# Gate products of the recurrent branch: stacked hi and lo fp32r products of a 64-channel block in place of fp32 products with block diagonal weights

## The chip, the cores and the metric

The kernel runs on one core of one Trainium2 chip. The metric is the device time of one execution in microseconds. A time named here is either the median of three runs or that of one profiled execution, and the text says which.

## What is computed

The reference is one layer of a hybrid decoder for 1040 prompt tokens (16 meta tokens ahead of 1024) and, separately, for eight running sequences of one token each. The kernel handles them side by side as 1050 columns (two are padding). The part that matters here is the recurrent branch (RG-LRU): a short causal convolution gives `xc`; two gates r and i come from `xc` by small dense products inside blocks of 64 channels; then a linear recurrence runs along the tokens.

```python
def _rglru(x, h0, wa, ba, wx, bx, lam):
    xb = xf.reshape(B, T, RG_BLOCKS, RG_BW)          # 16 blocks of 64 channels
    r = sigmoid(einsum('btnc,ncd->btnd', xb, wa) + ba)
    i = sigmoid(einsum('btnc,ncd->btnd', xb, wx) + bx)
    log_a = -RG_C * r * softplus(-lam)
    a = exp(log_a)
    b = sqrt(-expm1(2.0 * log_a)) * (i * xf)
    b = b.at[:, 0].add(a[:, 0] * h0)
    _, h = associative_scan(_lin_comb, (a, b), axis=1)
```

Around it stand a gated linear attention branch (GLA) on 128-token chunks, the merge of both branches, and a gated feed-forward block. All weights and activations are fp32.

## The kernel before, in words

The layout has channels on the 128 partitions and tokens along the free axis, so 1024 channels are eight blocks of 128. The large weight matrices come in 149 units of 128 output channels by 1024 input channels. For each unit a weight tile is fetched (`w_raw`), ACT copies it to an fp32r tile `w_hi` (`w_high`, line 795), and DVE subtracts to get the rest, `w_lo` (`w_low`, line 1196). PE (`tile_products`, line 417) then adds up three fp32r products, hi by hi, hi by lo and lo by hi, for three column groups of 346 or 350 columns each. A unit's result lies in `acc0` or `acc1`, three PSUM banks each, which alternate from unit to unit; before a unit may start, its `acc` must have been read out (semaphore `acc_free`).

The change lies in a loop of eight turns, one for each block j of 128 channels of the recurrent branch. Each turn also does one 128-token chunk of GLA and one running sequence, cut into small pieces that PE does between the eight tiles of a unit. The order of each engine is written out by hand: PE's turn is in the loop over `NPAIR` behind `gate_product` (line 604), ACT's and DVE's are two functions that are both called `rg_body`. In one turn of before:

- PE does unit `U_RG` (the x of the recurrent branch, into acc1) and unit `U_RG+1` (its gelu partner, into acc0). Behind tiles 3 and 4 of the latter stand `O_pair` (GLA's outputs of heads 0 and 1, and of heads 2 and 3, into the banks `small6` and `small7`), behind tiles 6 and 7 the state products `dS_piece`. Then follow the r gate as three fp32 products into acc1 (line 608), a small column sum (`onorm_piece`, line 547), and the i gate as three fp32 products into acc0. The next turn's first unit goes into acc1 again.
- DVE evacuates the x unit into `rg_ext`, masks GLA's scores (line 1317), does three convolution steps (line 1443) on the tile that ACT started (line 995), subtracts the next weights (line 1196), copies both O results to SBUF (`o_copy`, line 1323), updates GLA's state (line 1330), sums the squares (line 1337), evacuates the gelu partner into `rg_gelu_ha` (line 1224), and finishes the state and another weight subtraction. At the start of a turn it scales the O of the chunk before (line 1344) and carries out the recurrence of the block before (`rg_tail_w`, `rg_tail_b`, `rg_tail_h`; the last product is line 1413).
- ACT does the exponentials of GLA and of the block before, starts the convolution (line 995), copies weights (line 795), squares O (line 895), and ends the turn with the gelu (line 1005), a weight copy, the tanh of r out of acc1 (line 1009, which frees acc1), a tanh on r (line 1013), the tanh of i out of acc0 (line 1017), a table load, and GLA's reciprocal root (lines 901 and 905).

The gate weights `gw` of a block are 128 by 256: for each of the two gates a 128 by 128 matrix with two 64 by 64 blocks on its diagonal and zeros elsewhere.

```python
unit(U_RG + 1, ..., 0, G_RG[0] + 2 * j, XH, XL, {
    ...
    3: [lambda: O_pair(0, sb6)], 4: [lambda: O_pair(1, sb7)],
    6: [lambda: dS_piece(sb6, n, PAIR, 0)], 7: [lambda: dS_piece(sb7, n, PAIR, 1)]})
pe.wait_ge(xc_step, 4 * j + 4)
gate_product(1, G_RG[1] + 2 * j + 1, 0)
onorm_piece(n, PAIR)
gate_product(0, G_RG[0] + 2 * j + 1, 1)
```

Of the kernel before, what the change touches and what calls it, by code (L numbers as in the profile page):

```python
# [93 lines left out]
def view3(t):  # L94

    return t.rearrange("p (a n) -> p a n", a=3)
# [16 lines left out]
def build(nc, I, O):  # L113
    ctx = ExitStack()
    with ctx:  # L115
# [31 lines left out]
        xc = nxt("rg_xc_h", C)  # L147
        rt = nxt("rg_r", C)
        it = nxt("rg_i_b", C)
        av = nxt("rg_a", C)  # L150
# [18 lines left out]
        gw = nxt("rg_gate_weights", 2 * P)  # L169
        sS = nxt("smp_state", H * DV)  # L170
        svb = nxt("smp_v_rows", D)
        svt = svb
# [6 lines left out]
        h0 = nxt("rg_h0", KB * NS)  # L179
        der = nxt("rg_derived", 5 * KB)  # L180
        gbz = nxt("gla_bias", H)
        sqk = nxt("smp_qk", 8 * NS)
        sdec = nxt("smp_decay", H * NS)
        srv = nxt("smp_rinv", H * NS)
# [17 lines left out]
        T = [at(f"tmp{i}", T0 + TB * i, C) for i in range(3)]  # L202
        sqsum = T[2]
        sq1 = (rt, it, av, th)

        act_bytes = (2 * GRP * CB + 31) // 32 * 32
        AH = at("act_hi", A0, 2 * GRP * C, F32R)
# [34 lines left out]
        def sem(n):  # L242
            return ctx.enter_context(nc.semaphore(n))
# [20 lines left out]
        def squares(w):  # L264
# [39 lines left out]
        xbias_ready, xc_step, rgo_kept, gelu_ready, th_ready, a_ready, a2_ready, w_ready, ml_done, m_ready = (  # L304
            sem(n) for n in ("xbias_ready", "xc_step", "rgo_kept", "gelu_ready", "th_ready", "a_ready",
                             "a2_ready", "w_ready", "ml_done", "m_ready"))
        ix_ready, b_ready, h_step, ha_ready, ha_stored = (
            sem(n) for n in ("ix_ready", "b_ready", "h_step", "ha_ready", "ha_stored"))

# [101 lines left out]
        def _(pe):  # L411
# [189 lines left out]
                                              sqk[:, bass.ds(h * NS + j, 1)], start=True, stop=True)  # L601
                mm.then_inc(so_mm, 1)

            def gate_product(g, n_grp, half):

                pe.wait_ge(acc_free[g], n_grp)
                for n in range(3):
                    mm = nc.tensor.matmul(accv[g][:, n], gw[:, half * P:(half + 1) * P], xc[:, n * NW:(n + 1) * NW],
                                          start=True, stop=True)
                mm.then_inc(gate_mm, 1)  # L610

            with pe.Fori(0, NPAIR) as j:
                n = j + 1
                zn = j + 2

                def zg_pair():
                    pe.wait_ge(ones_done, 1)
                    pe.wait_ge(olog_done, n)
                    for h in range(H):  # L620
                        mm = nc.tensor.matmul(sb6[:, h * PAIR:(h + 1) * PAIR], wg[0:R2, h * DK:(h + 1) * DK],
                                              glr[0:R2, bass.ds(NMETA + PAIR * j, PAIR)], start=True, stop=True)
                    mm.then_inc(zg_mm, 1)

# [12 lines left out]
                unit(U_RG + 1, nth(U_RG + 1, 2, j), 0, G_RG[0] + 2 * j, XH, XL, {  # L637
                    1: [lambda: keT_piece(n, PAIR, so_ready, j + 1), lambda: A_piece(n, PAIR, z_ready, zn + 1)],
                    3: [lambda: O_pair(0, sb6)], 4: [lambda: O_pair(1, sb7)],
                    6: [lambda: dS_piece(sb6, n, PAIR, 0)], 7: [lambda: dS_piece(sb7, n, PAIR, 1)]})  # L640
                pe.wait_ge(xc_step, 4 * j + 4)
                pe.wait_ge(gwt_loaded, 16 * j + 16)
                gate_product(1, G_RG[1] + 2 * j + 1, 0)
                pe.wait_ge(S_ready, 2 * n + 1)
                onorm_piece(n, PAIR)
                gate_product(0, G_RG[0] + 2 * j + 1, 1)

            def onorm_samples():

# [129 lines left out]
        def _(act):  # L779
# [4 lines left out]
            def plain():  # L784

                act.wait_ge(ones_done, 1)
# [190 lines left out]
            def rg_body(j, first, last):  # L978
# [11 lines left out]
                if not last:  # L990
# [4 lines left out]
                nc.scalar.activation(xc, ext[:, 3:3 + C], ACT.Identity, scale=par("w3", j), bias=par("b", j))\  # L995
                    .then_inc(xbias_ready, 1)
                w_high(U_RG + 2, 2, j)
                act.wait_ge(sS_ready, j + 1)
                act.dma_start(O["gla_sample"][j], sS).then_inc(sS_stored, 16)
                if not last:  # L1000
                    rg_prefetch(j)
                o_square(n, PAIR, NMETA + PAIR * j, 0)
                o_square(n, PAIR, NMETA + PAIR * j, 1)
                act.wait_ge(acc_free[0], G_RG[0] + 2 * j + 1)
# [1 line left out]
                w_high(U_RG + 3, 2, j)  # L1006
                plain()
                act.wait_ge(gate_mm, 2 * j + 1)
                nc.scalar.activation(view3(rt), accv[1], ACT.Tanh, scale=0.5, bias=col(der, j)).then_inc(acc_free[1], 1)
                plain()  # L1010
                act.wait_ge(acc_free[1], G_RG[1] + 2 * j + 2)
                act.wait_ge(b_ready, j)
                nc.scalar.activation(th, rt, ACT.Tanh, scale=col(der, j + 4 * KB), bias=col(der, j + 4 * KB)).then_inc(th_ready, 1)
                plain()
                act.wait_ge(gate_mm, 2 * j + 2)
                act.wait_ge(h_step, 4 * j)
                nc.scalar.activation(view3(it), accv[0], ACT.Tanh, scale=0.5, bias=col(der, j + KB)).then_inc(acc_free[0], 1)
# [162 lines left out]
        def _(dve):  # L1180
# [234 lines left out]
            def rg_body(j, first):  # L1415
# [13 lines left out]
                nc.vector.tensor_copy(V3[:, :, bass.ds(NT + j, 1)], hd(sb7, 8, 1)).then_inc(so_ready, 1)  # L1429
                if not first:  # L1430
                    rg_tail_h(j - 1)
                    dve.wait_ge(xc_step, 4 * j)
# [3 lines left out]
                scores(n, PAIR)  # L1436
                c0 = NMETA + PAIR * j

                dve.wait_ge(xbias_ready, j + 1)
                dve.wait_ge(acc_free[1], G_RG[1] + 2 * j + 1)  # L1440
# [340 lines left out]
```

## Time and profile before

| | us |
|---|---|
| median of three runs | 1923.3 |
| the three runs | 1923.18, 1924.96, 1923.30 |
| the profiled execution, its own time | 1920.77 |
| its span, first to last instruction | 1919.0 |
| PE busy in it (matmuls) | 1890.9 |
| DVE busy | 921.1 |
| ACT busy | 565.7 |

The profile is of one execution. Busy times are shares of the whole span, over stages that differ; a matmul's displayed duration holds its way through the array, so that successive ones overlap, and the pace of PE is read from the distance of their starts. An fp32 matmul shows as two records of the same line. The timeline lists instructions by start and duration, and names in brackets what an engine waited for.

### The profile page before, as it was taken

Reading aid. Unit: us, or ns where it says so; the run is one execution under the profiler, and the core shown is the slowest. Engines: PE = TensorE matmul, PEld = TensorE weight load, DVE = VectorE, ACT = ScalarE, POOL = GpSimd, SP = SyncE. Lnnn points to the kernel's source line nnn. Section 1 sums busy time; section 2 is a strip of 40 time slices with the busy share of each in tenths; the row PEclk is TensorE's granted clock in tenths of the full one; section 3 lists DMA queues with packets and bytes.
Section 4 is the critical chain, followed back from the end, with each engine's and each line's share of the span. In section 5 each row is a group of like instructions: output and inputs, shape, how many; then the busy total and the mean of one; then the engine's idle time right before and its main releaser. Section 6 shows DMA issues by size and latency. Waiting matters only on the chain. (4 is left out here: it accounts for less than half of the span.)

```text
span 1919.0 us, 28820 instructions
## 1 busy us (share of the span) xinstructions
PE 1890.9 (99%) x11866; PEld 1860.3 (97%) x11866; DVE 921.1 (48%) x1067; ACT 565.7 (29%) x630; POOL 27.6 (1%) x24
## 2 busy tenths in 40 slices
PE   7999999999999999999999999999999999999998
PEld 6999899999999999999999999999999999999997
DVE  6221377788754222422244455545453545455455
ACT  5010256755642111211132332222121212131225
POOL 0000000000000000000000000000000000000032
PEclk9999999999999999999999999999999999999999
DMA  5221132223111111311131111111111111111112
GB/s 196 97 76 52 37 110 104 93 79 134 63 61 44 55 44 44 133 44 47 51 133 44 56 45 46 53 45 45 45 45 44 55 45 45 44 44 50 44 58 89
DMA packets 48234, 126.72 MB, mean 66 GB/s; under 512 B 7000, under 2 KB 20184, under 8 KB 48144
## 3 DMA queue, kind: packets, MB, share of 16 engines
q1 hardware_dynamic: 27808, 87.97, 13.6%
q10 hardware_dynamic: 20352, 37.64, 5.6%
q8 instruction: 62, 1.02, 0.2%
q14 instruction: 12, 0.10, 0.0%
HBM read 107.71 MB, written 18.14 MB: 66 GB/s over the span
## 5 line engine op out<-in xcount | busy, mean ns | idle before, releaser
L417 PE MATMUL acc<-xn_hi,w_hi 128*128 128x346 f32 (+1 forms) x2496 | 814.6, 326 | 2.5 <-issue 2.2
L417 PE MATMUL acc<-xn_lo,w_hi 128*128 128x346 f32 (+1 forms) x2496 | 803.6, 322 | 0.0
L417 PE MATMUL acc<-xn_hi,w_lo 128*128 128x346 f32 (+1 forms) x2496 | 801.5, 321 | 0.0
L417 PEld LDWEIGHTS acc<-xn_hi,w_hi 128*128 128x128 f32 x2496 | 470.9, 189 | 6.2 <-issue 3.4
L417 PEld LDWEIGHTS acc<-xn_lo,w_hi 128*128 128x128 f32 x2496 | 472.4, 189 | 1.5
L417 PEld LDWEIGHTS acc<-xn_hi,w_lo 128*128 128x128 f32 x2496 | 471.0, 189 | 0.0
L795 ACT ACTIVATE w_hi<-w_raw 128x1024 fp32r<-128x1024 f32 x149 | 156.4, 1050 | 460.2 <-PE acc L417 459.1
L1196 DVE TENSOR_TENSOR w_lo<-w_raw,w_hi 128x1024 fp32r<-128x1024 f32 x149 | 182.4, 1224 | 182.0 <-ACT w_hi L795 181.9
L417 PE MATMUL acc<-act_hi,w_hi 128*128 128x344 f32 x504 | 161.7, 321 | 2.6 <-DVE residual L1610 2.6
L417 PE MATMUL acc<-act_hi,w_lo 128*128 128x344 f32 x504 | 161.6, 321 | 0.0
L417 PE MATMUL acc<-act_lo,w_hi 128*128 128x344 f32 x504 | 161.6, 321 | 0.0
L1610 DVE TENSOR_TENSOR residual<-acc,residual 128x1032 f32<-128x1032 f32 x56 | 68.9, 1231 | 99.2 <-PE acc L417 99.2
L417 PEld LDWEIGHTS acc<-act_hi,w_hi 128*128 128x128 f32 x504 | 95.3, 189 | 4.6 <-DVE residual L1610 4.6
L417 PEld LDWEIGHTS acc<-act_lo,w_hi 128*128 128x128 f32 x504 | 95.1, 189 | 0.0
L417 PEld LDWEIGHTS acc<-act_hi,w_lo 128*128 128x128 f32 x504 | 94.8, 188 | 0.0
L1224 DVE TENSOR_TENSOR tmp<-acc,rms 128x1038 f32<-128x1038 f32 x24 | 29.7, 1239 | 134.8 <-PE acc L417 134.7
L1576 DVE TENSOR_TENSOR val_ext<-acc,rms 128x1038 f32<-128x1038 f32 x24 | 29.7, 1239 | 82.3 <-PE acc L417 82.3
L1115 ACT ACTIVATE gate_conv<-gate_ext,ffn_params 128x1032 f32<-128x1032 f32 x24 | 30.0, 1250 | 127.7 <-DVE gate_ext L1576 127.7
L1128 ACT ACTIVATE act_hi<-tmp 128x1032 fp32r<-128x1032 f32 x24 | 25.6, 1069 | 135.0 <-DVE tmp L1595 135.0
L1576 DVE TENSOR_TENSOR gate_ext<-acc,rms 128x1038 f32<-128x1038 f32 x24 | 29.7, 1239 | 72.2 <-PE acc L417 63.2
L1581 DVE SCALAR_TENSOR_TENSOR gate_conv<-gate_ext,ffn_params,gate_conv 128x1024 f32<-128x1024 f32 x48 | 61.5, 1282 | 2.9 <-DVE gate_conv L1581 0.9
L1581 DVE SCALAR_TENSOR_TENSOR tmp<-val_ext,ffn_params,tmp 128x1024 f32<-128x1024 f32 x48 | 61.5, 1282 | 2.8 <-DVE tmp L1581 0.2
(229 smaller groups left out, 2209.2 us busy)
## 6 DMA issues: line engine op xcount, KB each, us to landing
w_raw<-in_w SPq DMA_DIRECT2D x152, 512.0 KB, 3.5
ha_scratch<-rg_gelu_ha ACTq DMA_DIRECT2D x8, 519.0 KB, 2.7
h<-ha_scratch ACTq DMA_DIRECT2D x8, 519.0 KB, 6.1
residual<-in_x ACTq DMA_DIRECT2D x8, 519.0 KB, 6.4
gla_qk_pair<-qk_scratch ACTq DMA_DIRECT2D x8, 512.0 KB, 4.5
smp_v_rows<-smp_v_scratch ACTq DMA_DIRECT2D x8, 512.0 KB, 5.7
out_gla_sample<-smp_state ACTq DMA_DIRECT2D x8, 512.0 KB, 3.1
smp_state<-in_gla_state ACTq DMA_DIRECT2D x7, 512.0 KB, 4.9
```

What stands on the lines that cost most here:

```text
L417: mm = nc.tensor.matmul(acc[g][:, n, 0:cw], w[s][:, t * P:(t + 1) * P], x[:, c0 + n * cw:c0 + (n + 1) * cw], start=a, stop=z)
L795: nc.scalar.activation(whi[s], raw[s], ACT.Copy).then_inc(w_hi_done[s], 1)
L1115: nc.scalar.activation(cg[:, down_c], eg[:, 2 + D0:2 + D1], ACT.Identity, scale=fpr[:, bass.ds(2 * UB + F, 1)], bias=fpr[:, bass.ds(3 * UB ...
L1128: nc.scalar.activation(blkd(AH, half * GRP + f), act_t[:, down_c], ACT.Copy).then_inc(acth_done, 1)
L1196: nc.vector.tensor_tensor(wlo[s], raw[s], whi[s].bitcast(F32), ALU.subtract).then_inc(w_split[s], 1)
L1224: nc.vector.tensor_tensor(view3(out), acc[g][0:n_part, :, 0:cw], view3(rms[0:n_part, c0:c0 + 3 * cw]), ALU.mult)\
L1576: nc.vector.tensor_tensor(view3(e_t[:, 2 + L0:2 + L1]), accl[g], view3(rms[:, late]), ALU.mult).then_inc(acc_free[g], 1)
L1581: nc.vector.scalar_tensor_tensor(c_t[:, D0:NT], e_t[:, D0 + t:t + NT], fpr[:, bass.ds(t * UB + off_b + F, 1)], c_t[:, D0:NT], ALU.mult, AL ...
L1610: nc.vector.tensor_tensor(view3(blkd(X2, m)), accd[g], view3(blkd(X2, m)), ALU.add).then_inc(acc_free[g], 1)
```

## The change

The gate weights now come from the host in another arrangement: for each 64-channel block the weights of both gates stand side by side (64 input channels by 128 outputs), once on partitions 0 to 63 and once more on 64 to 127. For the second block the order of the two gates is turned round, and the bias of the i gate is stored with its halves swapped. ACT makes the fp32r tile `gwh` of them and DVE the rest `gwl`. From `xc` ACT makes the high part of the first block (partitions 0 to 63, tile `xsa`) and of the second (64 to 127, tile `xsb`), and DVE puts the low part of each on the other 64 partitions of the same tile. The two tiles lie over `rg_a` and `rg_mult`.

A gate product then gives both gates of one block: per column group one product of `gwh` over 128 partitions (hi weights by hi and lo activations at once) and one of `gwl` over the 64 partitions with the hi activations. The result has 64 partitions of r and 64 of i, so ACT reads it with four tanh on 64 partitions in place of two on 128.

`o_copy` moves from DVE to ACT, `O_pair` moves one tile later on PE, and DVE masks the scores ahead of the evacuation of the x unit instead of behind it.

```diff
+        xsa, xsb = at("xc_hi_lo", rt_at + 2 * xc_size, C, F32R), at("xc_lo_hi", rt_at + 3 * xc_size, C, F32R)
...
-            def gate_product(g, n_grp, half):
+            def gate_product(g, n_grp, xs, half, c0):
 
                 pe.wait_ge(acc_free[g], n_grp)
                 for n in range(3):
-                    mm = nc.tensor.matmul(accv[g][:, n], gw[:, half * P:(half + 1) * P], xc[:, n * NW:(n + 1) * NW],
-                                          start=True, stop=True)
+                    c = slice(n * NW, (n + 1) * NW)
+                    nc.tensor.matmul(accv[g][:, n], gwh[:, c0:c0 + P], xs[:, c], start=True, stop=False)
+                    mm = nc.tensor.matmul(accv[g][:, n], gwl[half, c0:c0 + P], xs[half, c], start=False, stop=True)
                 mm.then_inc(gate_mm, 1)
...
-                    3: [lambda: O_pair(0, sb6)], 4: [lambda: O_pair(1, sb7)],
+                    4: [lambda: O_pair(0, sb6)], 5: [lambda: O_pair(1, sb7)],
...
-                pe.wait_ge(xc_step, 4 * j + 4)
-                pe.wait_ge(gwt_loaded, 16 * j + 16)
-                gate_product(1, G_RG[1] + 2 * j + 1, 0)
+                pe.wait_ge(gw_split, j + 1)
+                pe.wait_ge(xs_split, 2 * j + 1)
+                gate_product(1, G_RG[1] + 2 * j + 1, xsa, slice(0, HP), 0)
                 pe.wait_ge(S_ready, 2 * n + 1)
                 onorm_piece(n, PAIR)
-                gate_product(0, G_RG[0] + 2 * j + 1, 1)
+                pe.wait_ge(xs_split, 2 * j + 2)
+                gate_product(0, G_RG[0] + 2 * j + 1, xsb, slice(HP, P), P)
...
                 w_high(U_RG + 2, 2, j)
+                act.wait_ge(gwt_loaded, 16 * j + 16)
+                nc.scalar.activation(gwh, gw, ACT.Copy).then_inc(gw_hi_done, 1)
...
+                o_copy(n, PAIR, NMETA + PAIR * j, 0, sb6)
+                o_copy(n, PAIR, NMETA + PAIR * j, 1, sb7)
+                act.wait_ge(xc_step, 4 * j + 4)
+                nc.scalar.activation(xsa[0:HP], xc[0:HP], ACT.Copy).then_inc(xs_hi_done, 1)
+                nc.scalar.activation(xsb[HP:P], xc[HP:P], ACT.Copy).then_inc(xs_hi_done, 1)
                 o_square(n, PAIR, NMETA + PAIR * j, 0)
                 o_square(n, PAIR, NMETA + PAIR * j, 1)
...
                 act.wait_ge(gate_mm, 2 * j + 1)
-                nc.scalar.activation(view3(rt), accv[1], ACT.Tanh, scale=0.5, bias=col(der, j)).then_inc(acc_free[1], 1)
+                act.wait_ge(h_step, 4 * j)
+                nc.scalar.activation(view3(rt[0:HP]), accv[1][0:HP], ACT.Tanh, scale=0.5, bias=der[0:HP, bass.ds(j, 1)])
+                nc.scalar.activation(view3(it[0:HP]), accv[1][HP:P], ACT.Tanh, scale=0.5, bias=der[HP:P, bass.ds(j + KB, 1)])\
+                    .then_inc(acc_free[1], 1)
...
-                o_copy(n, PAIR, c0, 0, sb6)
-                o_copy(n, PAIR, c0, 1, sb7)
+                dve.wait_ge(gw_hi_done, j + 1)
+                nc.vector.tensor_tensor(gwl, gw, gwh.bitcast(F32), ALU.subtract).then_inc(gw_split, 1)
+                dve.wait_ge(xs_hi_done, 2 * j + 1)
+                nc.vector.tensor_tensor(xsa[HP:P], xc[0:HP], xsa[0:HP].bitcast(F32), ALU.subtract).then_inc(xs_split, 1)
+                dve.wait_ge(xs_hi_done, 2 * j + 2)
+                nc.vector.tensor_tensor(xsb[0:HP], xc[HP:P], xsb[HP:P].bitcast(F32), ALU.subtract).then_inc(xs_split, 1)
                 state(n, PAIR, 0, sb6)
...
```

The order of ACT at the end of a turn, from the gelu's table load to the next one, before (`w_hi_55` is the second weight slot, `acc` either accumulator):

```order
L1005 ACT_TABLE_LOAD
L1005 ACTIVATE rg_gelu_ha<-rg_gelu_ha 128x1038
L795 ACTIVATE w_hi_55<-w_raw_53 128x1024
L1009 ACTIVATE rg_r<-acc,rg_derived 128x1050
L1013 ACTIVATE rg_mult<-rg_r,rg_derived 128x1050
L1017 ACTIVATE rg_i_b<-acc,rg_derived 128x1050
L1018 ACT_TABLE_LOAD
```

The same place now:

```order
L1026 ACT_TABLE_LOAD
L1026 ACTIVATE rg_gelu_ha<-rg_gelu_ha 128x1038
L804 ACTIVATE w_hi_55<-w_raw_53 128x1024
L1031 ACTIVATE rg_r<-acc,rg_derived 64x1050
L1032 ACTIVATE rg_i_b<-acc,rg_derived 64x1050
L1036 ACTIVATE rg_r<-acc,rg_derived 64x1050
L1038 ACTIVATE rg_i_b<-acc,rg_derived 64x1050
L1043 ACTIVATE rg_mult<-rg_r,rg_derived 128x1050
L1044 ACT_TABLE_LOAD
```

Two tanh of 128 partitions have become four of 64, and the tanh on r (`rg_mult<-rg_r`), which stood between the two, now stands behind all four.

The order of DVE from the end of the convolution to the evacuation of the gelu partner, before:

```order
L1447 COPY rg_last_columns<-rg_ext 128x13
L1196 TENSOR_TENSOR w_lo_58<-w_raw_54,w_hi_56 128x1024
L1323 COPY v_o<-small 128x4x128 x2
L1330 SCALAR_TENSOR_TENSOR gla_state<-gla_state,gla_exp_bc,small 128x256 x2
L1337 TENSOR_TENSOR gla_z_g_osq<-gla_z_g_osq 128x4x128
L1224 TENSOR_TENSOR rg_gelu_ha<-acc,rms 128x1038
```

And now:

```order
L1473 COPY rg_last_columns<-rg_ext 128x13
L1222 TENSOR_TENSOR w_lo_58<-w_raw_54,w_hi_56 128x1024
L1476 TENSOR_TENSOR rg_gate_weights_lo<-rg_gate_weights,rg_gate_weights_hi 128x256
L1478 TENSOR_TENSOR xc_hi_lo<-rg_xc_h,xc_hi_lo 64x1050
L1480 TENSOR_TENSOR xc_lo_hi<-rg_xc_h,xc_lo_hi 64x1050
L1356 SCALAR_TENSOR_TENSOR gla_state<-gla_state,gla_exp_bc,small 128x256 x2
L1363 TENSOR_TENSOR gla_z_g_osq<-gla_z_g_osq 128x4x128
L1250 TENSOR_TENSOR rg_gelu_ha<-acc,rms 128x1038
```

The two copies of O are gone from DVE, and three subtractions, one of gate weights and two of 64 partitions of activations, stand ahead of the state update and of that evacuation.

## Rows read from the trace of the kernel before

**Rows 1.** The page's part 1, PE: busy us (share of span) and instructions.

```profile
PE 1890.9 (99%) x11866; PEld 1860.3 (97%) x11866; DVE 921.1 (48%) x1067; ACT 565.7 (29%) x630; POOL 27.6 (1%) x24
```

**Rows 2.** Timeline of PE, end of one turn: start us, us, engine, line, operation.

```profile
480.10 0.32 PE L417 MATMUL acc<-xn_lo,w_hi 128*128 128x346 f32 x1
480.26 0.32 PE L417 MATMUL acc<-xn_hi,w_lo 128*128 128x346 f32 x1
...
483.57 1.93 PE L608 MATMUL acc<-rg_xc_h,rg_gate_weights 128*128 128x350 f32 x6
485.34 1.02 PE L547 MATMUL small<-gla_z_g_osq,ones 128*128 128x512 f32 x2
486.19 1.93 PE L608 MATMUL acc<-rg_xc_h,rg_gate_weights 128*128 128x350 f32 x6
487.69 0.59 PE L417 MATMUL acc<-xn_hi,w_hi 128*128 128x350 f32 x1
```

**Rows 3.** Timeline of ACT, the same turn.

```profile
472.32 1.26 ACT L995 ACTIVATE rg_xc_h<-rg_ext,params 128x1050 f32<-128x1050 f32 x1
...
484.25 1.07 ACT L1005 ACTIVATE rg_gelu_ha<-rg_gelu_ha 128x1038 f32<-128x1038 f32 x1 [1.51 <-DVE rg_gelu_ha L1224]
485.22 1.04 ACT L795 ACTIVATE w_hi<-w_raw 128x1024 fp32r<-128x1024 f32 x1
486.17 1.12 ACT L1009 ACTIVATE rg_r<-acc,rg_derived 128x1050 f32<-128x1050 f32 x1
487.47 1.27 ACT L1013 ACTIVATE rg_mult<-rg_r,rg_derived 128x1050 f32<-128x1050 f32 x1 [0.18 <-issue]
488.64 1.12 ACT L1017 ACTIVATE rg_i_b<-acc,rg_derived 128x1050 f32<-128x1050 f32 x1
489.78 1.28 ACT L1018 ACT_TABLE_LOAD   x1
```

**Rows 4.** Timeline of DVE, the same turn and the next one's O scaling.

```profile
455.06 1.23 DVE L1344 TENSOR_TENSOR v_o<-v_o,gla_qd 128x1024 f32 x1 [2.65 <-ACT gla_qd L905]
...
469.06 1.23 DVE L1413 TENSOR_TENSOR rg_gelu_ha<-rg_xc_h,rg_gelu_ha 128x1038 f32<-128x1038 f32 x1
...
471.37 0.75 DVE L1317 COPY_PREDICATED gla_scores<-causal_mask,small 128x512 f32<-128x512 int32 x1
...
478.20 1.22 DVE L1196 TENSOR_TENSOR w_lo<-w_raw,w_hi 128x1024 fp32r<-128x1024 f32 x1
479.34 1.28 DVE L1323 COPY v_o<-small 128x512 f32 x2
481.48 0.87 DVE L1330 SCALAR_TENSOR_TENSOR gla_state<-gla_state,gla_exp_bc,small 128x256 f32<-128x256 f32 x2 [0.86 <-PE small L540]
...
482.98 1.24 DVE L1224 TENSOR_TENSOR rg_gelu_ha<-acc,rms 128x1038 f32<-128x1038 f32 x1
...
493.05 1.23 DVE L1344 TENSOR_TENSOR v_o<-v_o,gla_qd 128x1024 f32 x1 [2.64 <-ACT gla_qd L905]
```

**Rows 5.** Lines L830 and L1230 (min/median/max ns), groups by line (busy us, mean ns).

```profile
L830 ACT ACTIVATE gla_low_rank<-acc x1: 1039/1039/1039, 24.1 to 24.1; 32x1050 f32<-32x1050 f32 x1
L1230 DVE TENSOR_TENSOR gla_low_rank<-gla_low_rank,rms x1: 1241/1241/1241, 39.3 to 39.3; 32x1050 f32<-32x1050 f32 x1
L875 ACT ACTIVATE gla_v_tokens<-small 128x512 f32<-128x512 f32 x16 | 9.4, 587 | 3.0 <-PE small L503 3.0
L1379 DVE TENSOR_SCALAR smp_state<-smp_state,smp_decay 128x256 f32<-128x256 f32 x32 | 9.1, 348 | 0.0
```

**Rows 6.** Stretches of 2 us: busy us by engine, granted TensorE clock, DMA share, GB/s.

```profile
210.00:212.00 2.00, 0.29 (x3) 0.28 (x4) 1.98 (x2) 1.32 (x2) 0.00 (x0) 1.00 0.00 0
...
218.00:220.00 2.00, 0.99 (x5) 0.98 (x5) 0.82 (x2) 0.26 (x1) 0.00 (x0) 0.62 0.00 0
...
222.00:224.00 2.00, 2.00 (x10) 1.94 (x9) 0.00 (x0) 0.60 (x1) 0.00 (x0) 0.50 0.00 0
224.00:226.00 2.00, 2.00 (x10) 2.00 (x10) 0.00 (x0) 0.00 (x0) 0.00 (x0) 0.67 0.70 231
```

More of the change, by code:

```diff
@@ L32 @@
 NMETA = 16
+HP = P // 2
 SEQ = 1024
@@ L147, in build @@
         xc = nxt("rg_xc_h", C)
+        rt_at, xc_size = off[0], (CB + 31) // 32 * 32
         rt = nxt("rg_r", C)
@@ L168, in build @@
         glr = nxt("gla_low_rank", C)
-        gw = nxt("rg_gate_weights", 2 * P)
+        gw_at = off[0]
+        gw, gwl = nxt("rg_gate_weights", 2 * P), at("rg_gate_weights_lo", gw_at, 2 * P, F32R)
         sS = nxt("smp_state", H * DV)
@@ L181, in build @@
         gbz = nxt("gla_bias", H)
+        gwh = nxt("rg_gate_weights_hi", 2 * P, F32R)
         sqk = nxt("smp_qk", 8 * NS)
@@ L306, in build @@
                              "a2_ready", "w_ready", "ml_done", "m_ready"))
+        gw_hi_done, gw_split, xs_hi_done, xs_split = (sem(n) for n in ("gw_hi_done", "gw_split", "xs_hi_done", "xs_split"))
+        r_ready = sem("r_ready")
         ix_ready, b_ready, h_step, ha_ready, ha_stored = (
@@ L890, in ke_tokens, with o_copy @@
                 nc.scalar.activation(bc[0:w, :], sb7[0:w, :], ACT.Copy).then_inc(keT_ready, 1)
+            def o_copy(n, w, c0, hh, bank):
+                plain()
+                act.wait_ge(O_mm, 2 * n + hh + 1)
+                nc.scalar.activation(V3[:, 4 * hh:4 * hh + 4, bass.ds(c0, w)], hd(bank, 4, w), ACT.Copy).then_inc(o_copied, 1)
             def o_square(n, w, c0, hh):
@@ L1008, in rg_body @@
                 act.wait_ge(gate_mm, 2 * j + 1)
-                nc.scalar.activation(view3(rt), accv[1], ACT.Tanh, scale=0.5, bias=col(der, j)).then_inc(acc_free[1], 1)
+                act.wait_ge(h_step, 4 * j)
+                nc.scalar.activation(view3(rt[0:HP]), accv[1][0:HP], ACT.Tanh, scale=0.5, bias=der[0:HP, bass.ds(j, 1)])
+                nc.scalar.activation(view3(it[0:HP]), accv[1][HP:P], ACT.Tanh, scale=0.5, bias=der[HP:P, bass.ds(j + KB, 1)])\
+                    .then_inc(acc_free[1], 1)
                 plain()
+                act.wait_ge(gate_mm, 2 * j + 2)
+                nc.scalar.activation(view3(rt[HP:P]), accv[0][HP:P], ACT.Tanh, scale=0.5, bias=der[HP:P, bass.ds(j, 1)])\
+                    .then_inc(r_ready, 1)
+                nc.scalar.activation(view3(it[HP:P]), accv[0][0:HP], ACT.Tanh, scale=0.5, bias=der[0:HP, bass.ds(j + KB, 1)])\
+                    .then_inc(acc_free[0], 1)
+                act.wait_ge(r_ready, j + 1)
                 act.wait_ge(acc_free[1], G_RG[1] + 2 * j + 2)
@@ L1013, in rg_body @@
                 nc.scalar.activation(th, rt, ACT.Tanh, scale=col(der, j + 4 * KB), bias=col(der, j + 4 * KB)).then_inc(th_ready, 1)
[L1014 to L1017, printed above, removed]
                 act.preload_act_table_set(LN_EXP)
@@ L1431, in rg_body @@
                     rg_tail_h(j - 1)
+                scores(n, PAIR)
+                if not first:
                     dve.wait_ge(xc_step, 4 * j)
@@ L1435, in rg_body @@
                 evacuate(U_RG, 2, j, 1, ext[:, 3:3 + C])
-                scores(n, PAIR)
-                c0 = NMETA + PAIR * j
                 dve.wait_ge(xbias_ready, j + 1)
@@ L1725 @@
     x = np.ascontiguousarray(tokens.T.reshape(KB, P, C))
-    vecs = [a["rg_conv_w"][0][i] for i in range(4)] + [a["rg_conv_b"][0], a["rg_ba"][0], a["rg_bx"][0],
+    vecs = [a["rg_conv_w"][0][i] for i in range(4)] + [a["rg_conv_b"][0], a["rg_ba"][0], a["rg_bx"][0].reshape(KB, 2, HP)[:, ::-1].reshape(-1),
             a["rg_lambda"][0], a["norm1_g"][0], a["gla_norm_g"][0].reshape(-1), a["norm2_g"][0], a["final_norm_g"]]
-    gates = np.zeros((KB, P, 2, P), f32)
-    for c, w in enumerate((a["rg_wa"][0], a["rg_wx"][0])):
-        w = w.reshape(KB, 2, 64, 64)
-        gates[:, 0:64, c, 0:64] = w[:, 0]
-        gates[:, 64:128, c, 64:128] = w[:, 1]
+    wa, wx = (a[n][0].reshape(KB, 2, HP, HP) for n in ("rg_wa", "rg_wx"))
+    pairs = np.stack([np.concatenate([wa[:, 0], wx[:, 0]], axis=2), np.concatenate([wx[:, 1], wa[:, 1]], axis=2)], axis=2)
+    gates = np.ascontiguousarray(np.concatenate([pairs, pairs], axis=1))
     t = np.arange(P)
```

## The prediction

> **What bounds the kernel now.** I read the page's busy times first: PE is busy 99% of the span [rows 1], so at first sight whatever shortens PE's stream shortens the run. That share is an average, so I then read one turn of the loop over the eight 128-channel blocks, where the change lies, on three timelines: PE, ACT, DVE. A turn takes 37.99 us: DVE scales the same O tile at 455.06 and again at 493.05 [rows 4]. PE has no idle mark in it. At the end of a turn come the two fp32 gate products [rows 2], then the next unit's first product, displayed at 487.69 but advancing only when the second gate product ends, about 487.95 (486.19 plus 1.77).
>
> The reader should now see how thin the cover is. That next unit accumulates into the same three banks (acc1) as the first gate product, so it waits until ACT has read the product out. ACT reads it at 486.17 for 1.12 us, done at 487.29 [rows 3]: 0.66 us before PE needs it. ACT is not late because the product is (it ended near 485.4) but because gelu and a weight copy stand ahead of the tanh in its queue: gelu starts at 484.25, when DVE's evacuation of 482.98 (1.24 us) ends [rows 3, 4]. Here, not in PE's busy share, a change of this loop is decided.
>
> **PE's products.** Each fp32 gate product (three column groups) takes 485.34 - 483.57 = 1.77 us of PE [rows 2]. It becomes six products at fp32r, which follow each other every 0.16 us (480.10 to 480.26 [rows 2]): 0.96 us. Saved: 0.8 us twice a turn, 1.6 us a turn, 12.8 us in all, if nothing else bound. The products over 64 rows have no row of their own; between no cost and one whole product's 0.16 I take 0.16, as the other products. Moving the O products one tile later adds no PE work.
>
> **What partitions cost.** Much of the added work is on 64 partitions instead of 128. The nearest rows say that this buys nothing: ACT needs 1.04 us for 32x1050, DVE 1.24 us for 32x1050 [rows 5], beside 1.12 and 1.24 for full tiles of that length [rows 3, 4]. So I price each by its columns. The lower bound, half price, is a rival below.
>
> **DVE's part of the turn.** From its first weight subtraction (478.20) to the evacuation that ACT's gelu waits for (482.98) DVE now spends 4.78 us, including a wait for PE ahead of 481.48 [rows 4]. The change takes out the two O copies and puts in one subtraction of gate weights (128x256, 0.35 by the nearest row [rows 5]) and two of 64x1050, 1.24 long and about 1.16 apart (successive DVE instructions start some 0.08 earlier than their durations say: 478.20 to 479.34 for 1.22 [rows 4]). New stretch: 1.14 + 0.35 + 1.16 + 1.16 + 1.50 (481.48 to 482.98) = 5.31, **0.53 us later**. ACT's high parts are in time: convolution ends by 478.20, copy of 1.07, so 479.3; the first subtraction starts at 479.7. That the scores now precede the evacuation of the x block costs nothing: 469.06 + 1.15 + 0.67 + 1.24 = 472.12, and ACT starts on that tile only at 472.32 [rows 3, 4].
>
> **ACT's part.** The O copies (about 0.59 each [rows 5]), the high part of the gate weights and the two high parts of the activations lie in ACT's idle time between 474.5 and 484.2; the two high parts end near 480.3 (two pitches of about 0.97 and a tail behind 478.3), two squares of the O copies' length near 481.5, in time for DVE's sum at about 482.8. Behind the gelu nothing covers: two tanh become four. Pitch of one: 1.12 less the 0.10 by which ACT's successive starts overlap (484.25 to 485.22 for 1.07 [rows 3]), 1.02. From the first tanh to the table load: before 489.78 - 486.17 = 3.61; now 4 x 1.02 + 1.28 = 5.36, **1.75 us more**. The table load, the logarithm and the reciprocal root follow, and DVE's next turn begins with them (493.05).
>
> **The new turn.** Evacuation, gelu, tanhs, reciprocal root, O scaling, recurrence, convolution, evacuation: a ring through DVE and ACT in which PE does not occur. Before, PE set its pace and the ring had little to spare. Now it takes 37.99 + 0.53 + 1.75 = 40.27 us, 2.3 longer, and eight turns add **18 us**. PE's 1.6 us become waiting, with the 2.3: it frees acc1 only after the second tanh. In the ring's own times gelu starts at 484.78, the tanhs at 486.70 and 487.72, acc1 is free at 488.84. PE, which in the new rhythm starts its unit 1.3 us earlier against DVE, finishes its gate products near 485.7. So I expect **one wait of about 3.1 us per turn ahead of the next unit**, and some 0.8 us of smaller ones. The extra waits on the split operands cost PE nothing: their low part is done at 480.95, PE gets there at 482.3.
>
> **The clock.** Such a wait may lower PE's clock. The trace has one fall inside its work: after a wait that left PE busy only 0.29 of the 2 us from 210 on, followed by small matmuls and shorter waits, the granted clock was 0.62, 0.50, 0.50 and 0.67 in the four stretches from 218 to 226 [rows 6], that is 1.2 instead of 2.4 GHz. That is 3.4 us of full-speed work, about 3.1 where PE had any. The stretch of the wait itself still has 1.00. So eight waits cost between 0 and 8 x 3.1 = 25 us. I take five falls of half that length, since dense products surround the wait, less 0.15 of slack between PE and the ring: 5 x 1.4 = **7 us**.
>
> Sum: the profiled execution took 1920.8 us (span 1919.0), and 1920.8 + 18 + 7 = 1945.8. The median of the runs shown is 2.5 higher, so as a median **1948 us**. The stage behind the loop gets its input 25 us later and otherwise runs as before.
>
> **The rivals.** *No fall of the clock*: the 3.1 us waits pass as the one at 210 at first did; then only the ring counts, 1923.3 + 18 = 1941. For it: that wait; against: this one is longer and comes every turn.
>
> *A full fall in every turn*: each wait costs 3.1 and PE's start joins the ring: 1923.3 + 18 + 25 = 1966. Against: the one fall of the trace needed a longer sparse stretch than one wait. The Trainium skill, TensorE: Matmul & The Clock Gate, section "HAM oscillation — how this bites in real kernels", describes loops whose PE waits in each pass and restarts at the lower clock in each pass; by it this rival's 1966 would hold, and no run here shows such a loop yet.
>
> *Half price on 64 partitions*, the case that ends not slower: four tanh then take as long as two, the two subtractions save what they add, DVE's evacuation stays at 482.98 because PE's unit ends just ahead of it, and acc1 is back at 486.17 + 0.46 + 0.56 = 487.19 (a half-price pitch, then a half-price duration). PE starts at 487.3 instead of 487.95, 0.65 a turn: 1923.3 - 5 = 1918. It decides as soon as the two tanhs together take less than 1.7 us. Even then gelu and weight copy stand ahead, so the full 12.8 us (1910.5) are out of reach. Against it: [rows 5].
>
> **How the numbers follow.** Forecast with some falls 0.55, no fall 0.26, a fall in every turn 0.12, half price 0.05, the remaining 0.02 unnamed. The range reaches from 1934 (no fall, with the ring 0.9 us per turn shorter than worked out) to 1962 (falls nearly every turn, most of the full length); the half-price case and the upper part of the full falls are left out. A measurement of this kernel tells 0.2%, about 4 us, from no change: faster 0.04, same 0.03, slower 0.93.
>
> **What would show it.** Right: turns of 40 us or more between two scalings of O; PE idle for some 3 us ahead of the first product of a unit in each turn, released by ACT's second tanh; gate products 0.16 us apart; DVE's evacuation behind the two 64x1050 subtractions; clock stretches of 0.50 behind some of the waits. Wrong: 64-row tanhs well under 1.1 us, or PE without idle marks in the loop, would overturn the ring; turns of 40 us with the clock at 1.00 throughout would leave 1941; turns near 43 us would mean that the clock costs more than the ring.

## The result and the profile after the change

The changed kernel takes 1957.98 us (median of six runs, 1951.41 to 1959.14), the kernel before 1923.16 us beside it: a ratio of 1.018 (95% interval 1.0167 to 1.0193), 34.8 us slower. The forecast was 1948 us with a range to 1962. The profiled execution took 1956.45 us, its span is 1954.6 us: 35.6 longer than the span before.

First the page of the changed kernel, part 1 (busy us, share of the span, instructions), the answer to [rows 1]:

```profile
PE 1912.7 (98%) x11866; PEld 1872.4 (96%) x11866; DVE 933.0 (48%) x1075; ACT 612.4 (31%) x686; POOL 27.6 (1%) x24
```

PE is busy for 98% of the span instead of 99% and for 21.8 us more than before. By that page alone one would still call PE the bound. The turn of the loop says otherwise. On DVE's timeline of the changed kernel (start us, us, engine, line, operation, xcount, in brackets the idle time before it and its releaser), from one scaling of O to the next, the answer to [rows 4]:

```profile
356.11 1.23 DVE L1370 TENSOR_TENSOR v_o<-v_o,gla_qd 128x1024 f32 x1 [4.92 <-ACT gla_qd L919]
...
379.26 1.22 DVE L1222 TENSOR_TENSOR w_lo<-w_raw,w_hi 128x1024 fp32r<-128x1024 f32 x1
...
381.20 1.25 DVE L1478 TENSOR_TENSOR xc_hi_lo<-rg_xc_h,xc_hi_lo 64x1050 fp32r<-64x1050 f32 x1 [0.38 <-ACT xc_hi_lo L1021]
382.48 1.25 DVE L1480 TENSOR_TENSOR xc_lo_hi<-rg_xc_h,xc_lo_hi 64x1050 fp32r<-64x1050 f32 x1
383.76 0.87 DVE L1356 SCALAR_TENSOR_TENSOR gla_state<-gla_state,gla_exp_bc,small 128x256 f32<-128x256 f32 x2
...
385.15 1.23 DVE L1250 TENSOR_TENSOR rg_gelu_ha<-acc,rms 128x1038 f32<-128x1038 f32 x1
...
397.49 1.23 DVE L1370 TENSOR_TENSOR v_o<-v_o,gla_qd 128x1024 f32 x1 [4.92 <-ACT gla_qd L919]
```

The turn has grown from 37.99 to 41.38 us (356.11 to 397.49). From the weight subtraction at 379.26 to the evacuation that gelu waits for (385.15) DVE needs 5.89 us; before it needed 4.78 [rows 4]. On ACT's timeline of the same turn, the answer to [rows 3]:

```profile
379.60 0.60 ACT L904 ACTIVATE v_o<-small 128x512 f32 x1 [1.33 <-PE small L538]
380.10 1.07 ACT L1021 ACTIVATE xc_hi_lo<-rg_xc_h 64x1050 fp32r<-64x1050 f32 x1
381.19 1.08 ACT L1022 ACTIVATE xc_lo_hi<-rg_xc_h 64x1050 fp32r<-64x1050 f32 x1
...
388.34 1.11 ACT L1031 ACTIVATE rg_r<-acc,rg_derived 64x1050 f32<-64x1050 f32 x1
389.46 1.13 ACT L1032 ACTIVATE rg_i_b<-acc,rg_derived 64x1050 f32<-64x1050 f32 x1
390.62 1.14 ACT L1036 ACTIVATE rg_r<-acc,rg_derived 64x1050 f32<-64x1050 f32 x1
...
394.22 1.28 ACT L1044 ACT_TABLE_LOAD   x1
395.51 0.69 ACT L915 ACTIVATE gla_qd<-small,consts 128x512 f32<-128x512 f32 x1
```

From the first tanh to the table load ACT needs 5.88 us instead of 3.61 [rows 3]. DVE's 1.11 and ACT's 2.27 make 3.38, and the turn is 3.39 longer: the whole lengthening lies on these two engines. But PE is not outside the ring. The subtraction at 381.20 waits 0.38 us for ACT's high part (380.10), which stands behind the second O copy (379.60), which waits for PE's O product. PE comes to that product through one unit and most of the next, which it could begin only when ACT let it. In a turn behind a fall of the clock the same wait is longer:

```profile
423.29 1.25 DVE L1478 TENSOR_TENSOR xc_hi_lo<-rg_xc_h,xc_hi_lo 64x1050 fp32r<-64x1050 f32 x1 [1.11 <-ACT xc_hi_lo L1021]
```

So a ring through ACT, PE and DVE closes last here; without PE this turn would be at most 0.38 us shorter. PE's timeline, one turn later, shows the gate products and what comes behind them, the answer to [rows 2]:

```profile
425.74 0.51 PE L616 MATMUL acc<-xc_hi_lo,rg_gate_weights_hi 128*128 128x350 f32 x1
426.18 0.42 PE L617 MATMUL acc<-xc_hi_lo,rg_gate_weights_lo 64*128 64x350 f32 x1
426.53 0.42 PE L616 MATMUL acc<-xc_hi_lo,rg_gate_weights_hi 128*128 128x350 f32 x1
...
432.75 0.51 PE L424 MATMUL acc<-xn_hi,w_hi 128*128 128x350 f32 x1 [1.75 <-ACT rg_i_b L1032]
```

The six products of a gate are 0.35 us apart, not 0.16, and PE then waits 1.75 us for ACT's second tanh. Over the stretch from 260 to 560 us the list of waits (total us, times, longest) has this one first:

```profile
PE acc L424 <- ACT rg_i_b L1032: 12.2, 7, 1.8
```

Last the clock, as stretches of the changed kernel (length, PE busy with its instructions, granted clock, DMA share, GB/s):

```profile
200.00:260.00 60.00, 56.70 (x347) 0.91 0.21 71
260.00:554.00 294.00, 280.30 (x1695) 0.97 0.25 85
554.00:600.00 46.00, 44.26 (x245) 0.93 0.17 58
600.00:1900.00 1300.00, 1295.94 (x8144) 1.00 0.16 54
```

In the same stretches the kernel before has 0.94, 1.00, 1.00 and 1.00. The loss of full-speed time beyond that kernel's is about 60 x 0.03 + 294 x 0.03 + 46 x 0.07 = 13.8 us; the mean clocks give the same (0.989 of 1954.6 against 0.996 of 1919.0). Part of it falls into time in which PE would have waited anyway. Around the wait of 432.75 the two-us stretches read:

```profile
430.00:432.00 2.00, 1.00 (x3) 1.00 0.00 0
432.00:434.00 2.00, 1.25 (x5) 0.74 0.41 104
434.00:436.00 2.00, 2.00 (x9) 0.50 0.39 158
436.00:438.00 2.00, 2.00 (x14) 0.91 0.00 0
```

Here the fall comes as PE resumes, and after 436 it recovers: 1.7 us of full speed lost, half of the fall in [rows 6]. Such falls lie behind six of the eight turns (264, 392, 432, 472, 518 and 558 us). Two of them, from 472 and 558 on, are longer and begin inside the wait (0.81 from 558 to 560, where the wait ends at 560.14); each loses 3.4 us of full speed, as much as the fall in [rows 6].

**Where the 35.6 us lie.** The first O scaling of the loop starts 7.6 us later than before (272.72 against 265.13). Of that, 1.9 come from the start of the kernel and 1.9 from the fall at the loop's entry, which both kernels have and which is longer here (216 to 230 us instead of 218 to 226 [rows 6]); the other 3.8 are the first turn. The 3.8 ahead of it are not the change's, as the section on the prediction shows. The seven turns up to the last scaling (566.29 against 530.29) add 28.4: 7 x 3.40 = 23.8 of ring, 4.6 of clock. What follows the last scaling is 0.4 shorter. So the ring takes about 27.6 us (with DVE's short wait behind PE's O product in it), the clock some 6.5, of which 1.9 ahead of the loop, and the start 1.9. In the turns behind a fall the clock's part reaches the turn as DVE's wait of 1.1 to 1.4 us for ACT's high part, in place of 0.35 to 0.38.

### The profile page after: what moved, and what is told of

Read it like the earlier page. It is cut to its first block and busy times, and to the rows that moved or that the text cites. A ratio compares the mean times of both kernels' runs of the same rounds, so it can differ in the third digit from the quotient of the medians.

```text
span 1954.6 us, 28902 instructions
## 1 busy us (share of the span) xinstructions
PE 1912.7 (98%) x11866; PEld 1872.4 (96%) x11866; DVE 933.0 (48%) x1075; ACT 612.4 (31%) x686; POOL 27.6 (1%) x24
## 3 DMA queue, kind: packets, MB, share of 16 engines
q8 instruction: 62, 1.02, 0.2%
## 5 line engine op out<-in xcount | busy, mean ns | idle before, releaser
L424 PEld LDWEIGHTS acc<-xn_hi,w_hi 128*128 128x128 f32 x2496 | 474.7, 190 | 20.0 <-ACT rg_i_b L1032 13.8
```

The costliest lines, as they stand in the source:

```text
L424: mm = nc.tensor.matmul(acc[g][:, n, 0:cw], w[s][:, t * P:(t + 1) * P], x[:, c0 + n * cw:c0 + (n + 1) * cw], start=a, stop=z)
```

## The experiments

The theory: the ring through DVE and ACT sets the turn, because half a tile costs as much as a whole one; PE's pace does not matter, but its wait costs clock. The rivals: PE's slow gate products set the turn; the wait ahead of the next unit does; the clock does.

**1. All 128 rows in every gate product.** The products of low weights take all rows, which adds the product of the two low parts:

```diff
-                    mm = nc.tensor.matmul(accv[g][:, n], gwl[half, c0:c0 + P], xs[half, c], start=False, stop=True)
+                    mm = nc.tensor.matmul(accv[g][:, n], gwl[:, c0:c0 + P], xs[:, c], start=False, stop=True)
```

> The changed kernel, with the low-weight product of each gate over all 128 partitions instead of 64 (it then also adds low weights by low activations). Ring theory (the turn is set by the ring through DVE and ACT): the gate product falls from 2.21 us to about 0.96, PE's wait ahead of the next unit grows from 1.75 us to about 3, the turn stays 41.4 us (within 0.3) where the clock is at 1.00, median between 1950 and 1962. Rival (the slow pace of the 64-row products is the loss): 2.5 us less per turn, 20 in all, median near 1938.

Measured: 1956.96 us (1955.12 to 1960.73), ratio 1.0175 (1.0158 to 1.0192), within the interval of the changed kernel. PE's timeline of this kernel:

```profile
300.81 0.51 PE L616 MATMUL acc<-xc_hi_lo,rg_gate_weights_hi 128*128 128x350 f32 x1
301.16 0.32 PE L617 MATMUL acc<-xc_hi_lo,rg_gate_weights_lo 128*128 128x350 f32 x1
301.32 0.33 PE L616 MATMUL acc<-xc_hi_lo,rg_gate_weights_hi 128*128 128x350 f32 x1
...
307.83 0.66 PE L424 MATMUL acc<-xn_hi,w_hi 128*128 128x350 f32 x1 [2.98 <-ACT rg_i_b L1032]
```

With as many products and the same columns the distance is 0.16 us behind the first. PE finishes earlier and waits longer, 2.98 us instead of 1.75. In the profiled execution, the slowest of the four (1960.73 us), every turn has a fall of the clock (0.92 or 0.96 in every 42 us of the loop), so the turns compare with those of the changed kernel that have one: 41.97 to 42.09, or 43.07 to 43.19 with a longer fall (there 42.00 to 42.11 and 43.20), and 41.38 for the last turn (there 41.40), which is 0.75 us shorter than the others in the kernel before. No turn here shows the length without a fall. From the first gate product to the next unit PE takes 7.02 us (300.81 to 307.83) as in the changed kernel 7.01 (425.74 to 432.75): the pace of the gate products is not the bound, and the whole gain of about 2.4 us became wait. The run does not test the rest of PE's work, which lies between ACT's release and the O product. The serial products of the changed kernel come from their 64 rows: the weight loads no longer run ahead. Whether the alternation with 128 rows does it or the 64 rows by themselves, no run separates. PE's weight loads of the changed kernel show it, each with an idle time that no semaphore explains:

```profile
511.83 0.19 PEld L616 LDWEIGHTS acc<-xc_hi_lo,rg_gate_weights_hi 128*128 128x128 f32 x1 [0.17 <-issue]
512.19 0.18 PEld L617 LDWEIGHTS acc<-xc_hi_lo,rg_gate_weights_lo 64*128 64x128 f32 x1 [0.17 <-issue]
```

**2. The split tanhs alone, in the kernel before.** Each of the two gate tanhs is written as two of 64 partitions; nothing else changes:

```diff
-                nc.scalar.activation(view3(rt), accv[1], ACT.Tanh, scale=0.5, bias=col(der, j)).then_inc(acc_free[1], 1)
+                nc.scalar.activation(view3(rt[0:64]), accv[1][0:64], ACT.Tanh, scale=0.5, bias=der[0:64, bass.ds(j, 1)])
+                nc.scalar.activation(view3(rt[64:P]), accv[1][64:P], ACT.Tanh, scale=0.5, bias=der[64:P, bass.ds(j, 1)]).then_inc(acc_free[1], 1)
```

and the same for `it` on `accv[0]`.

> The kernel before, with only each gate tanh of 128 partitions split into two of 64. Ring theory: each half takes as long as the whole, so acc1 comes back about 1.1 us later (0.66 us of cover) and the ring gets 2.3 us longer, of which about 1 is covered: turn between 38.5 and 39.4 us instead of 37.99, median 1927 to 1935. Rival (half the partitions, half the time): turn 37.99, median 1923.

Measured: 1941.8 us (1939.25 to 1943.44), ratio 1.0098 (1.0081 to 1.0114), more than expected. ACT's timeline of this kernel:

```profile
422.10 1.12 ACT L1009 ACTIVATE rg_r<-acc,rg_derived 64x1050 f32<-64x1050 f32 x1
423.23 1.13 ACT L1010 ACTIVATE rg_r<-acc,rg_derived 64x1050 f32<-64x1050 f32 x1
...
425.82 1.13 ACT L1018 ACTIVATE rg_i_b<-acc,rg_derived 64x1050 f32<-64x1050 f32 x1
426.97 1.14 ACT L1019 ACTIVATE rg_i_b<-acc,rg_derived 64x1050 f32<-64x1050 f32 x1
428.12 1.28 ACT L1020 ACT_TABLE_LOAD   x1
```

A tanh on 64 partitions takes 1.12 to 1.14 us, one on 128 took 1.12 [rows 3]: no part of the price goes with the partitions, and the half-price rival has fallen. The first tanh and the table load are now 6.02 us apart, 2.41 more than before, and the turns are 40.11 to 40.31 instead of 37.99 (41.17 in the two with a fall of the clock, 39.30 in the last, which before took 37.24). I had expected less because I counted only the wait for acc1. The second return from ACT to PE is in the list of waits:

```profile
PE small L621 <- ACT gla_qd L901: 6.4, 7, 1.0
```

The next turn's gate logits (L621) go into a bank that ACT's logarithm (L901) must have read, and the logarithm stands behind the tanhs and the table load. PE is in the ring here too: DVE's state update still waits 0.69 us for PE's state product (at 417.39). This edit alone gives more than half of the slowdown. DVE's part was not put into the kernel before by itself.

**3. The first two tanhs ahead of gelu.** In the changed kernel, the two tanhs that free acc1 are moved ahead of gelu and the weight copy (here as the lines that move):

```diff
-                act.wait_ge(acc_free[0], G_RG[0] + 2 * j + 1)
-                nc.scalar.activation(gy[:, late], gy[:, late], ACT.Gelu_apprx_tanh).then_inc(gelu_ready, 1)
-                w_high(U_RG + 3, 2, j)
...
                     .then_inc(acc_free[1], 1)
+                act.wait_ge(acc_free[0], G_RG[0] + 2 * j + 1)
+                nc.scalar.activation(gy[:, late], gy[:, late], ACT.Gelu_apprx_tanh).then_inc(gelu_ready, 1)
+                w_high(U_RG + 3, 2, j)
```

> The changed kernel, with ACT's first two gate tanhs ahead of the gelu and the weight copy instead of behind them. Ring theory: acc1 is free before PE ends its second gate product, PE's wait ahead of the next unit goes from 1.75 us to under 0.3, the granted clock stays at 1.00 in the loop, the ring sheds about 1.6 us because two tanhs now run while DVE evacuates: turn near 39.8 us, median near 1940. Rival (the 64-row products' pace and the clock): the ring does not matter, turn at PE's own 38.9 us, median near 1930. Rival (clock falls alone): turn still 41.4, median 1952.

Measured: 1982.42 us (1981.1 to 1983.85), ratio 1.0313 (1.0296 to 1.033): a miss, for a reason outside the question. ACT's timeline of this kernel:

```profile
395.42 1.28 ACT L1028 ACT_TABLE_LOAD   x1 [2.56 <-PE acc L617]
...
399.01 1.28 ACT L1032 ACT_TABLE_LOAD   x1
...
405.95 1.28 ACT L1044 ACT_TABLE_LOAD   x1
```

A tanh that comes first gets another table set than gelu's, so each turn now has three loads of 1.28 us instead of two, and turns last 45 to 47 us. The same with edit 1 added:

> The edits of e1 and e2 together. Ring theory: as e2, turn 39.5 to 39.8 us, median 1937 to 1940, because PE has time to spare. Rival (PE's product pace): 2.5 us a turn below e2, median near 1920.

gave 1975.93 us (1967.96 to 1977.47), ratio 1.0267 (1.024 to 1.0294), with turns of 43.64 to 45.13: again the table, so neither run says what the order alone is worth.

**4. The same order with the table named.** As edit 3, with gelu's set loaded by name ahead of the first tanh, so that ACT loads two tables per turn as in the changed kernel:

```diff
+                act.preload_act_table_set("gelu_apprx_tanh_and_others")
```

 Theory (e2 lost its gain to two table loads of 1.28 us in the ring): one table load less per turn, turn near 39.9 us, PE's wait for acc1 under 0.3 us, but a wait of about 1 us ahead of the gate logits (line L629) for ACT's logarithm; median 1938 to 1946. Rival (tanhs ahead of the gelu are slower for another reason): turn over 41.4 us, median over 1958.

Measured: 1959.05 us (1957.3 to 1965.17; the profiled execution is the slowest), ratio 1.0181 (1.0166 to 1.0197): no gain, where I expected one. The wait for acc1 is gone from the list, and another has its place:

```profile
PE small L629 <- ACT gla_qd L915: 16.6, 7, 2.4
```

It is the gate logits' wait of experiment 2, now 2.4 us in every turn. ACT's timeline says why (the first tanh, released by PE's last gate product, and the logarithm):

```profile
433.71 1.13 ACT L1029 ACTIVATE rg_r<-acc,rg_derived 64x1050 f32<-64x1050 f32 x1 [1.29 <-PE acc L617]
...
442.96 0.69 ACT L915 ACTIVATE gla_qd<-small,consts 128x512 f32<-128x512 f32 x1
```

From the evacuation (432.82) to the logarithm ACT's tail takes 10.14 us, in the changed kernel 10.36 (385.15 to 395.51): the moved tanhs must wait 1.29 us for PE, so the order saves 0.22 us. PE's gate product now stands in the ring as well, every turn has a fall (granted clock 0.92 in each 42 us), and DVE waits 1.48 us for ACT's high part, released by PE's late O product; turns last 44.25 us. Hence the wait for acc1 is a symptom: what holds PE is ACT's whole tail, through acc1 or through the logits, whichever holds it longer.

**5. Products in place of the wait.** In the changed kernel four of the six products of the second gate are run once more ahead of the real ones, so that PE works for 1.4 us where it would wait:

```diff
-                for n in range(3):
+                for n in list(range(again)) + [0, 1, 2]:
...
-                gate_product(0, G_RG[0] + 2 * j + 1, xsb, slice(HP, P), P)
+                gate_product(0, G_RG[0] + 2 * j + 1, xsb, slice(HP, P), P, 2)
```

> The changed kernel, with the first four products of the second gate product of each turn done once more ahead of it (1.4 us of PE that nothing waits for; results are overwritten by the same values). Theory that the clock falls because of PE's wait ahead of the next unit: the wait shrinks from 1.75 us to under 0.5, the granted clock stays at 1.00 in the loop behind its first turn, all turns become 41.4 us, median 5 to 8 us lower, 1950 to 1953. Rival (the falls come from elsewhere, or cost nothing): falls as before, median 1956 to 1960. Rival (PE's product time counts): 1.4 us more per turn, median near 1969.

Measured: 1950.65 us (1946.64 to 1950.97), ratio 1.0134 (1.0119 to 1.015): 7.3 us faster than the changed kernel, with more work. Three of its turns by stretch (columns as in the clock's stretches above):

```profile
386.00:428.00 42.00, 40.85 (x249) 1.00 0.27 91
428.00:470.00 42.00, 41.66 (x247) 0.96 0.26 91
470.00:512.00 42.00, 41.66 (x247) 0.96 0.27 91
```

Falls are left in two of the seven turns instead of five, the mean clock rises from 0.989 to 0.993 (13.6 us of full speed lost instead of 21.5), and turns without a fall stay at 41.34 to 41.40 us, as the ring says. So the clock's share is real and of about this size, and the ring's share does not depend on it. Falls also differ between executions: one of the changed kernel's six runs took 1951.41 us at a mean clock of 0.993, the other five 1956.45 to 1959.14 at 0.988 or 0.989. All four runs here lie below those five, and the intervals of the two ratios do not overlap.

**6. Splitting hi and lo without splitting partitions.** From the kernel before: the block diagonal weights stay, and each fp32 product becomes three fp32r products of 128 rows (hi x hi, hi x lo, lo x hi). One ACT copy and one DVE subtraction of 128x1050 make the parts, and each gate keeps its one tanh. The O copies on ACT, `O_pair` one tile later and the earlier mask are as in the change, but the second O copy stands behind the high part:

```diff
-                    mm = nc.tensor.matmul(accv[g][:, n], gw[:, half * P:(half + 1) * P], xc[:, n * NW:(n + 1) * NW],
-                                          start=True, stop=True)
+                    c = slice(n * NW, (n + 1) * NW)
+                    nc.tensor.matmul(accv[g][:, n], gwh[:, c0:c0 + P], xsa[:, c], start=True, stop=False)
+                    nc.tensor.matmul(accv[g][:, n], gwh[:, c0:c0 + P], xsb[:, c], start=False, stop=False)
+                    mm = nc.tensor.matmul(accv[g][:, n], gwl[:, c0:c0 + P], xsa[:, c], start=False, stop=True)
...
+                o_copy(n, PAIR, NMETA + PAIR * j, 0, sb6)
+                act.wait_ge(xc_step, 4 * j + 4)
+                nc.scalar.activation(xsa, xc, ACT.Copy).then_inc(xs_hi_done, 1)
+                o_copy(n, PAIR, NMETA + PAIR * j, 1, sb7)
...
+                nc.vector.tensor_tensor(xsb, xc, xsa.bitcast(F32), ALU.subtract).then_inc(xs_split, 1)
```

> The hi and lo split of the change, but with the old block diagonal weights and all 128 partitions: three fp32r products per gate and column group, one copy and one subtraction of 128x1050, two tanhs of 128 partitions, and ACT's copy of the second O half behind its high part of the activations. Ring theory: the ring is no longer than before, no 64-row product and no 64-partition instruction is left, each gate product takes 9 x 0.16 = 1.44 us instead of 1.77, of which PE keeps what acc1's return allows: turn 37.4 to 37.6 us, median 1918 to 1921, 2 to 5 below the kernel before. Rival (splitting the activations on ACT and DVE costs the ring as much as in the change): turn over 38.5, median over 1927.

Measured: 1918.7 us (seven runs, 1916.55 to 1919.02) against 1923.47, ratio 0.9974 (0.9963 to 0.9985): 4.8 us below the kernel before. ACT's and DVE's timelines of one turn:

```profile
478.65 1.08 ACT L1020 ACTIVATE xc_hi<-rg_xc_h 128x1050 fp32r<-128x1050 f32 x1 [0.93 <-DVE rg_xc_h L1465]
479.64 0.58 ACT L904 ACTIVATE v_o<-small 128x512 f32 x1
```

```profile
455.42 1.23 DVE L1364 TENSOR_TENSOR v_o<-v_o,gla_qd 128x1024 f32 x1 [2.65 <-ACT gla_qd L919]
...
478.61 1.22 DVE L1216 TENSOR_TENSOR w_lo<-w_raw,w_hi 128x1024 fp32r<-128x1024 f32 x1
...
482.84 1.24 DVE L1244 TENSOR_TENSOR rg_gelu_ha<-acc,rms 128x1038 f32<-128x1038 f32 x1
...
492.92 1.23 DVE L1364 TENSOR_TENSOR v_o<-v_o,gla_qd 128x1024 f32 x1 [2.64 <-ACT gla_qd L919]
```

and PE's, at the end of the second gate product and the start of the next unit:

```profile
485.92 0.32 PE L617 MATMUL acc<-xc_lo,rg_gate_weights_hi 128*128 128x350 f32 x1
486.08 0.32 PE L618 MATMUL acc<-xc_hi,rg_gate_weights_lo 128*128 128x350 f32 x1
...
487.22 0.43 PE L424 MATMUL acc<-xn_hi,w_hi 128*128 128x350 f32 x1
```

The products are 0.16 us apart, but the first of each gate is followed only after 0.34 and 0.56 us, so the gates take 1.65 and 1.86 us and not the 1.44 that I expected. From the last state product of a turn to the first small product of the next unit PE needs 6.21 us (445.07 to 451.28) instead of 6.70 (444.72 to 451.42), 0.49 less, and that is the turn's gain: 37.50 instead of 37.99. DVE's stretch is 0.55 shorter than before (482.84 - 478.61 = 4.23), ACT's tail as long as before. PE has no wait in the loop, starts the next unit on time at 487.22, and the loop's clock is 1.00 throughout. More products than the change, yet faster: what the change lost was lost on DVE and ACT. Against the change two things differ at once, the full tiles and the place of the second O copy, by which DVE's subtraction no longer waits for ACT; the second alone in the changed kernel was not tried.

## Why the prediction was right, and which terms were mis-sized

**The bound.** Right in the main: what the half tiles cost on DVE and ACT decides, and the gate products' pace does not matter. Experiment 1 shortens the gate products by about 2.4 us per turn and leaves the time alone; experiment 2 puts the tanhs into the kernel before and makes it 18.9 us slower than that kernel beside it. Wrong in one step: a ring "in which PE does not occur". The path that closes last runs from ACT's tail through PE's work up to the O product, the O copy and ACT's high part to DVE's subtraction, which waits 0.35 to 0.38 us there in turns without a fall and 1.1 to 1.4 behind one, 6.8 us in the seven turns. So PE's clock lengthens a turn although PE waits in it.

**PE's products.** Wrong: I priced the 64-row product at 0.16 us, as the others, and each gate product at 0.96 us, a saving of 1.6 per turn. Alternating with 128-row products they are 0.35 us apart and a gate product takes 2.2 us (425.74 to 427.94), longer than the fp32 one. It cost nothing because PE had to wait anyway, but it is why the forecast wait of 3.1 us was 1.75; with the even distance of experiment 1 it is 2.98.

**What partitions cost.** Right: full price on 64 partitions, on both engines.

**DVE's part.** Mis-sized: +1.11 instead of +0.53. Two reasons. The subtraction at 381.20 waits 0.38 us for ACT's high part, which starts only at 380.10 because the second O copy ahead of it in ACT's queue waited for PE's O product until 379.60; I had ACT's high part in time. This makes 0.45. And the 64-partition subtractions follow each other after 1.28 us, not the 1.16 that I had from full tiles: 0.24 more, less 0.11 ahead of the evacuation.

**ACT's part.** Mis-sized: +2.27 instead of +1.75. Four tanhs of 64 partitions follow each other after 1.12 to 1.16 us; I had estimated 1.02 from the overlap of a gelu with a weight copy; no two full tanhs follow each other in the trace.

**The ring.** So 3.40 instead of 2.3 us per turn, about 27.6 us instead of 18. The forecast of 25 us came 10 short of the measured 34.8, and these two terms over eight turns are 8.8 of it.

**The clock.** Right in kind and near in size: I forecast five falls worth 7 us. Six came; five of them cost 4.6 us in the seven turns, and without most of them experiment 5 is 7.3 us shorter. That the number came so near is in part luck, for the falls differ between executions of the same kernel. The rival with a fall in every turn did not come about in the changed kernel, though it did in the profiled executions of experiments 1 and 4. The Trainium skill, TensorE: Matmul & The Clock Gate, section "HAM oscillation — how this bites in real kernels", has the lower clock return in every pass of a loop whose PE waits; here it did so in six of eight passes at waits near 1.75 us, and in every pass where they were 2.98.

**What I left out.** The 1.9 us at the start and the longer fall at the loop's entry, another 1.9, have no term in my sum, and the runs show that they belong to the execution and not to the change: a small O scaling ahead of the loop (128x128) starts at 220.38 before and at 224.15 in the changed kernel, but between 220.54 and 226.34 in experiments 1, 3, 4 and 5, whose edits act only later. The clock from 200 to 260 us varies with it (0.97 in experiment 4, 0.91 in the changed kernel, 0.89 in experiments 5 and 6). And ACT's return to PE through the logarithm and the logits, which I named only as what follows the tanhs, binds in experiments 2 and 4.

## What to carry to other kernels

Cutting a tile in two along partitions doubles the number of instructions on ACT and DVE, and each half costs as much as the whole: count such instructions on the ring that sets the turn before counting what TensorE saves. When an engine is 99% busy, look for the return that lets it go on and for its slack (here 0.66 us) before taking its work as the bound, and follow that path through every engine: here it leads from ACT through PE to an O copy and back to DVE. A split into high and low parts can be had with full tiles, as experiment 6 shows, and an order on ACT must be read together with the tables that it makes ACT load.

## What was not expected of the hardware

- fp32r products of 64 and 128 rows in turn are 0.35 us apart for 350 columns; with 128 rows throughout, 0.16 behind the first (experiment 1). In the alternation each weight load starts with its own product, after 0.17 us of idle time that no semaphore explains. That rows of different number hinder the early load is a reading that fits; no run has products of 64 rows behind each other, and which part of the hardware does it stays open.
- Successive instructions on half the partitions do not overlap on ACT and DVE as full tiles do. ACT's high part takes 1.07 or 1.08 us either way, but the next instruction starts 1.09 us behind the half tile (380.10 to 381.19) and 0.99 behind the full one (478.65 to 479.64). DVE's subtraction of a half tile is followed after 1.28 us; the full one of experiment 6 after 1.16 at the least. The tanhs of half a tile follow each other after 1.12 to 1.16; for full ones no row shows it.
- A tanh ahead of gelu loads another table set than gelu's, 1.28 us more per turn at each change of set, unless the set is named.
- Filler work can pay: with 1.4 us of repeated products per turn the mean clock was 0.993 instead of 0.989, and the median 7.3 us shorter.
